# Differential attention of a decoder trunk: scaling the second map and adding the maps as one VectorE operation

## The reference, cut to what matters

```python
s = jnp.einsum('bqhme,bkhme->bhmqk', q2, k2).astype(jnp.float32) * (A_HD ** -0.5)
s = jnp.where(dist >= 0, s + bias[:, None], -jnp.inf)
p = jax.nn.softmax(s, axis=-1)
w = p[:, :, 0] - lam * p[:, :, 1]
return jnp.einsum('bhqk,bkhe->bqhe', w, v.astype(jnp.float32))
```

## Time and profile before

| what | value |
|---|---|
| median of three runs | 3593.33 us |
| the profiled execution, its own time | 3596.45 us |
| its span | 3594.9 us |
| granted PE clock, mean over the span | 0.969 |
| busy over the span: PE, DVE, ACT, POOL | 91%, 53%, 38%, 14% |

### The profile page before, as it was taken

One profiled execution on the slowest core, in us unless ns is written; L12 is line 12 of the kernel. 1 busy time (PEld: TensorE's weight loads), 2 busy tenths in 40 slices (PEclk: granted clock), 3 DMA queues, 4 the chain that ended last, 5 costly groups with the idle time before them and its releaser, 6 DMA issues. The chain is left out here.

```text
span 3594.9 us, 58426 instructions
## 1 busy us (share of the span) xinstructions
PE 3268.0 (91%) x19347; PEld 3022.6 (84%) x19347; DVE 1909.9 (53%) x4454; ACT 1378.7 (38%) x2979; POOL 516.2 (14%) x397
## 2 busy tenths in 40 slices
PE   6999999688889998688599699999999999999997
PEld 5999999577779997344488599999999999999997
DVE  5222222466668875233598465376366537636754
ACT  5111111377766775222344233333333333333332
POOL 0011011144430001233254000010010001001000
PEclk9999999899999999899799899999999999999999
DMA  4333334633537666999476676467447647644342
GB/s 131 112 106 104 108 121 132 174 72 84 111 77 167 168 171 184 283 318 302 165 246 208 186 230 210 118 214 231 142 149 252 197 123 225 218 147 145 117 116 83
DMA packets 642920, 597.48 MB, mean 166 GB/s; under 512 B 42729, under 2 KB 565442, under 8 KB 637570
## 3 DMA queue, kind: packets, MB, share of 16 engines
q1 hardware_dynamic: 610806, 461.86, 45.1%
q10 hardware_dynamic: 12814, 70.05, 5.6%
q0 software_dynamic: 19104, 63.06, 5.3%
HBM read 492.42 MB, written 169.68 MB: 184 GB/s over the span
## 5 line engine op out<-in xcount | busy, mean ns | idle before, releaser
L2358 DVE TENSOR_TENSOR ff_wl<-ff_wr,ff_wh 128x1024 fp32r<-128x1024 f32 (+2 forms) x380 | 404.1, 1079 | 283.4 <-ACT ff_wh L2290 282.3
L2290 ACT ACTIVATE ff_wh<-ff_wr 128x1024 fp32r<-128x1024 f32 (+2 forms) x380 | 349.5, 939 | 245.7 <-PE ff_d L2218 123.5
L450 PE MATMUL pj_acc<-hT_h,pj_wh 128*128 128x416 f32 x960 | 339.6, 354 | 10.1 <-POOL pj_wl L367 10.1
L450 PE MATMUL pj_acc<-hT_l,pj_wh 128*128 128x416 f32 x960 | 337.5, 352 | 0.0
L2216 PE MATMUL ff_g<-ff_hh,ff_wh 128*128 128x416 f32 x880 | 309.7, 352 | 26.8 <-DMA ff_hh<-scratch_h2T 23.7
L2216 PE MATMUL ff_u<-ff_hh,ff_wh 128*128 128x416 f32 x880 | 310.8, 353 | 16.5 <-DVE ff_wl L2358 16.5
L2216 PE MATMUL ff_d<-ff_ah,ff_wh 128*128 128x416 f32 x880 | 313.2, 356 | 9.4 <-DVE ff_wl L2358 9.4
L2218 PE MATMUL ff_d<-ff_ah,ff_wl 128*128 128x416 f32 x880 | 310.8, 353 | 0.0
L2218 PE MATMUL ff_g<-ff_hh,ff_wl 128*128 128x416 f32 x880 | 310.6, 353 | 0.0
L2218 PE MATMUL ff_u<-ff_hh,ff_wl 128*128 128x416 f32 x880 | 310.4, 353 | 0.0
L2217 PE MATMUL ff_g<-ff_hh,ff_wh 128*128 128x416 f32 x880 | 308.4, 350 | 0.1
(11 more groups left out here) (266 smaller groups left out, 7079.0 us busy)
## 6 DMA issues: line engine op xcount, KB each, us to landing
ff_wr<-in_w_gate SPq DMA_DIRECT2D x110, 512.0 KB, 4.1
ff_wr<-in_w_up SPq DMA_DIRECT2D x110, 512.0 KB, 5.0
bx_kca<-in_cache_a_k SPq DMA_DIRECT2D x128, 256.0 KB, 10.5
sa_vca<-in_cache_a_v POOLq DMA_DIRECT2D x128, 256.0 KB, 7.2
out<-in_cache_win_k ACTq DMA_DIRECT2D x64, 511.0 KB, 4.7
out<-in_cache_win_v ACTq DMA_DIRECT2D x64, 511.0 KB, 4.7
ff_wr<-in_w_down SPq DMA_DIRECT2D x80, 384.0 KB, 4.0
ff_wr<-in_w_down SPq DMA_DIRECT2D x80, 320.0 KB, 3.5
```

Source lines behind the costliest of these rows:

```text
L450: m = pe.matmul(acc[g][:, 0:PG], weights[:, k, c], part[:, c, cols], start=start, stop=stop)
L2290: act.activation(wh[:, slot, 0:size], wr[:, slot, 0:size], ACT.Copy).then_inc(w_hi, 1)
L2358: dve.tensor_tensor(wl[:, slot, 0:size], wr[:, slot, 0:size], wh[:, slot, 0:size].bitcast(F32), ALU.subtract).then_inc(w_lo, 1)
```

## The change

`scale` and the POOL block are gone, and with them the semaphore `p2_ok`. In their place DVE does `combine(x-1)` right behind `factors(x-1)`: p1 = p2 * c2 + p1, one `scalar_tensor_tensor` over all the tile's keys, in place in p1. It raises `w_ok`, for which the same consumers wait as before: `turn` on PE, and DVE's own `add_bias` and `factors` for the buffers `p2` and `c2`.

```diff
+            def combine(x):
+                n = keys(x)
+                dve.wait_ge(c2_ok, raised(x + 1))
+                dve.scalar_tensor_tensor(p1[:, x % R1, 0:n], p2[:, x % R2, 0:n], c2[:, x % 4:x % 4 + 1], p1[:, x % R1, 0:n],
+                                         ALU.mult, ALU.add).then_inc(w_ok, 1)
+
@@ DVE's list
                         negate_max(x)
                         if x >= 1:
                             factors(x - 1)
+                            combine(x - 1)
                 if x == NX:
                     factors(x - 1)
+                    combine(x - 1)
...
-        @block.gpsimd
-        def _(pool):
-            for x in range(NX):
-                n = keys(x)
-                w, y = p1[:, x % R1, 0:n], p2[:, x % R2, 0:n]
-                pool.wait_ge(p2_ok, raised(x + 1))
-                pool.tensor_tensor(w, w, y, ALU.add).then_inc(w_ok, 1)
...
-            def scale(x):
-                y = p2[:, x % R2, 0:keys(x)]
-                act.wait_ge(c2_ok, raised(x + 1))
-                act.activation(y, y, ACT.Copy, scale=c2[:, x % 4:x % 4 + 1]).then_inc(p2_ok, 1)
-
@@ ACT's list
             for x in range(NX + LAG):
                 n = parts(x - LAG)
-                if 0 <= x - 2 < NX:
-                    scale(x - 2)
```

More of the change, by code:

```diff
@@ L527, in attend_a @@
         o_out = [s.sem(f"o_out{i}") for i in range(2)]
-        (scored, biased, max_ok, exp_ok, rl_ok, c2_ok, p2_ok, w_ok, turned, wt_act, wt_dve, pv, o_ok) = (
-            s.sem(n) for n in ("scored", "biased", "max_ok", "exp_ok", "rl_ok", "c2_ok", "p2_ok", "w_ok", "turned",
+        (scored, biased, max_ok, exp_ok, rl_ok, c2_ok, w_ok, turned, wt_act, wt_dve, pv, o_ok) = (
+            s.sem(n) for n in ("scored", "biased", "max_ok", "exp_ok", "rl_ok", "c2_ok", "w_ok", "turned",
                                "wt_act", "wt_dve", "pv", "o_ok"))
```

## The result

The changed kernel took 3632.58 us (median of four runs, 3629.0 to 3635.0), the kernel before 3594.34 us in the same comparison (four runs). The ratio is 1.0109 with a 95% interval of 1.0096 to 1.0122: slower by 38 us. The forecast was 3632 us. The sum behind that number was not as good as the number, as the stretches show.

A forecast was written before the change was run, and what follows sets the result against it. In attention A's tiles 4 to 15 PE leads and DVE follows closely. Floor 29.8, unusable waits 10.5, between heads 0 and end -1.4 sum to 38.9 us, giving 3632 us; range 3609 to 3666 us.

The forecast's parts named there:

- DVE's list paces the tiles 4 to 15: Attention A, long stretches: DVE would use up its waits and be the later engine, busy 95% or more in tiles 9-11.
- The price of combine: DVE's new operation: 1.04 ns an element plus 0.22 us, about 1.3 us in the mean, 86 us busy.
- If every wait of DVE in these tiles is used up ... a head grows by 16.7 less its waits: Floor for tiles 4 to 15 (head 0: 9 to 15): 4.9, 8.5, 8.6 and 7.8 us by head, together 29.8 us.
- Neither sets the pace in these tiles: Tiles 4 to 15: removing ACT's 77.1 us and POOL's 161.1 us gives back only part of DVE's 8.9 us waits.
- PE's stop before a group that DVE copies: Waits DVE can't use: about 5 us in head 2, 1.5 in head 1, 1 in others; 10.5 us with tiles 8-11.
- the walk: Tile 13 stepped through from combine's end: DVE waits nothing, 0.3 or 1.45 us as it copies group 2, 1 or 0.
- rival B: Tiles 4 to 15: DVE's waits stay and combine comes on top; 3654 us, to 3680 with PE's lower clock; chance 0.18.
- Between heads: Three passages: products 0.8 us later each, 2.4 us, against 2.4 us from one c2 operation; sum 0, bounds -6 to +6.
- The tiles before head 0's query load cost nothing, the end gives 1.4 us: Head 0's early growth, some 3 us, only shortens the load wait; without POOL the stage's end comes 1.4 us sooner.
- The checks named: Changed profile: DVE's exponential waits under 25 us, no score waits in head 3's long tiles, PE's score-bank waits new and large.
- C: Rival: the loop through factors, scale and POOL paces the tiles, DVE's 90.6 us of waits cover combine; 3585 us, chance 0.09.
- D: Rival: combine runs at two elements a cycle, halving 1.04 ns; 3602 us, chance 0.07.

The follow-up runs named there:

- e4: The changed kernel with combine over only the first half of a tile's keys; 3596.64 us (ratio 1.0005).
- e11: The changed kernel with every copy of transposed maps on ACT, and finish on ACT too; 3553.72 us (ratio 0.9906).
- e7: The kernel before without ACT's scale pass, the factor left out and POOL's sum waiting for c2 alone; 3576.06 us (ratio 0.9948).
- e1: The changed kernel with every copy of transposed maps on ACT, none on DVE; 3562.87 us (ratio 0.9927).
- e10: The kernel before, scale on ACT and sum on POOL, with every copy of transposed maps on ACT; 3585.13 us (ratio 0.9980).
- e2: The changed kernel with DVE's copies counted anew in each head, every head as head 0; 3610.71 us (ratio 1.0071).
- e3: The changed kernel with DVE's copies in every head as in head 2, group 0 in the long tiles; 3658.81 us (ratio 1.0189).
- e6: The kernel before with only POOL's sum moved to DVE, behind the first map's adds, scale staying on ACT; 3617.86 us (ratio 1.0068).
- e12: e11 with combine in pieces of 512 keys, each releasing its own group of transposes; 3552.02 us (ratio 0.9891).
- e5: The changed kernel with PE repeating score chunk 3's two matmuls three more times in head 2's tiles 12 to 15; 3627.37 us (1.0117).

## Why the prediction was right or wrong

- *DVE's list paces the tiles 4 to 15.* Right in heads 0, 1 and 3, and shown: DVE is busy 96 to 98% of them (86% in head 2). In head 3 its waits fell from 8.9 to 0.5 us, and the length of combine (e4) and the 0.26 us of finish (e11) come out again in tiles 4 to 11.
- *The price of combine.* Right: 1.352 us in the mean, 86.5 us in all; I had about 1.3 and 86. The c2 operation starts at 1064.30 in head 3, combine at 1064.56 and the next add 2.00 us after that, with 1792 keys; the sum had 0.26 and 2.00 us:

```profile
1064.30 0.22 DVE L738 SCALAR_TENSOR_TENSOR aa_c<-aa_ll,aa_nlam,aa_rl 128x1 f32<-128x1 f32 x1
1064.56 2.08 DVE L744 SCALAR_TENSOR_TENSOR aa_p<-aa_p,aa_c 128x1792 f32<-128x1792 f32 x1
1066.56 0.68 DVE L715 CUSTOM_DVE_ANT_0 aa_p<-aa_sc,aa_bias 128x512 f32<-128x512 f32 x1
```

- *"If every wait of DVE in these tiles is used up ... a head grows by 16.7 less its waits".* This term was too large: 4.9, 8.5 and 7.8 us for heads 0, 1 and 3 as a floor, and measured 2.7, 6.8 and 4.6 in all. I took the idle time that the waits view doesn't list (0.15 us a tile) as fixed and the busy time as incompressible. Both gave way. An add that follows another at once takes 0.61 us of the list; one followed by a wait shows 0.69, and it is the whole 0.69 that counts as busy. In head 3, 16.7 us of list went into 4.6 us of growth, so 12.2 us were found, more than the 10.7 us of idle time: busy time grew by 13.6 us (54.31 to 67.88), and the idle time fell by 9.0. All of the growth lies in tiles 4 to 11 (34.25 to 38.82 us); the long tiles took 30.78 us before and 30.76 after, because before something else held them up (the next point).
- *"Neither sets the pace in these tiles", of ACT and POOL.* Wrong for ACT. Without its pass the tiles 4 to 15 were 4.1, 2.4 and 4.0 us shorter in heads 1 to 3 (e7), although has only 1.2 us of waits for exponentials, and PE's matmuls waited 0.8 us for copies by ACT in head 3's long tiles. What I had left out are the waits of PE's weight loads (PEld). In the kernel before, head 3, the first row is of tiles 12 to 15, the second of tiles 4 to 11:

```profile
PEld aa_ob L673 <- ACT aa_wt L802: 2.6, 7, 0.7
```

```profile
PEld aa_tb L660 <- POOL aa_p L773: 3.3, 4, 1.2
```

  The same rows in e7: none, and 1.4 us. So the products stood behind ACT's copies, and the transposes behind POOL's sum, which itself waited for ACT's pass. How the 4.0 us divide between the two no run separates, because e7 also lets POOL start sooner. The long tiles of e1 and e10 fit this: 28.8 us without such waits for ACT, 30.8 us with 3.0 us of them.
- *PE's stop before a group that DVE copies.* Right in kind, head by head, before any run (e2 and e3 confirm it), and near in size in head 2 (+16.6, forecast +14.4). But there two errors met: the order costs 11.1 us (81.03 against 69.93 in e2), where I had about 5, and the list 5.5 us (69.93 against 64.44), where I had 8.6. In head 1 the order costs 1.7 us (71.80 against 70.07), where I had 1.5. The stop itself is in the timeline of PE, tile 13 of head 2:

```profile
942.89 1.16 PE L673 MATMUL aa_ob<-aa_vv,aa_wt 128*128 128x128 f32 x8 [2.04 <-DVE aa_wt L724]
943.80 0.91 PE L648 MATMUL aa_sc<-bx_kk,aa_qq 128*128 128x512 f32 x2
944.51 0.84 PE L660 MATMUL aa_tb<-bx_ident,aa_p 128*128 128x128 f32 x3
945.01 1.20 PE L648 MATMUL aa_sc<-bx_kk,aa_qq 128*128 128x512 f32 x2
946.00 1.80 PE L673 MATMUL aa_ob<-aa_vv,aa_wt 128*128 128x128 f32 x8
```

  What the walk lacked is what follows the stop: a pair of score matmuls takes 1.20 instead of 0.71 us and eight products 1.80 instead of 1.06. I had the lower clock only as part of rival B. DVE's waits in head 2's long tiles were 2.0 us a tile in the mean (1.36, 2.87, 2.83, 1.00), not 1.45.
- *Between heads: 0.* Wrong, +5.3 us: -0.4, +1.9 and +3.8. The sum left out which groups DVE copies: in e2, where every head has head 0's pattern, the passages differ from the kernel before by -0.4, -0.6 and +0.1 us. The first passage came out as the walk had it: factors 1.7 us earlier in the iteration, the copy at 766.33 behind 2.27 us of combine, and the products 0.7 us later in the passage (I had 0.8). PE's stop before that copy grew from 3.91 to 6.29 us, since PE also got there sooner. The one c2 operation that took 2.64 us has none like it now (all 64 have a mean of 220 ns).

```profile
767.07 2.08 PE L673 MATMUL aa_ob<-aa_vv,aa_wt 128*128 128x128 f32 x8 [6.29 <-DVE aa_wt L724]
```

- *The tiles before head 0's query load cost nothing, the end gives 1.4 us.* Right: the wait for the load fell from 7.69 to 5.4 us on DVE, the tiles up to 8 came out 0.6 us shorter, and the end gave 1.8.
- *The total.* 33.6 us in the stage against 38.9, and 4.0 us behind it in the profiled pair, which is within the spread of the later stages. The mechanism was right, but that the forecast met the median to 1 us was luck: three heads were overrated by about 12 us, and head 2, the passages and the later stages made up 11 to 12.
- *The checks named.* DVE's wait for exponentials under 25 us, no waits for scores in head 3, the growth of PE's waits: right. But the larger new wait of PE is for DVE's copies (17.1 to 49.1 us), not for the scores' banks (11.5 to 23.9, of which 10.6 are the wait at the start of the stage in both).
- *The rivals.* C, that the loop through scale and POOL is the limit, falls as a forecast: the loop's waits did not cover combine. It holds in part for the kernel before, where e7 shows that ACT's pass, and with it the start of POOL's sum, cost 4.0 us in head 3. Taking the sum off POOL does not pay by itself: with it alone moved (e6) the kernel is slower by 0.7%. B, waits unchanged, holds in head 2 alone. D falls by the price.

The version that beats both kernels is e12 or e11: 3552 and 3554 us, 1.1 and 0.9% under the kernel before.

## What to carry to other kernels

A share of busy time below 100% in an in-order list is not slack that a new long instruction can use: ask what the engine does for others behind it. Here a costly part was a 0.6 us copy queued behind a 2 us sum, for which another engine stood still, and its place in a rotation decided 9.6 us a head. Work taken off an engine (ACT's 77 us) is worth more once something is given to it in exchange: moved together with the copies, the same change is about 20 us faster instead of 38 us slower. To see who holds PE up, read the waits of its weight loads too, and not those of its matmuls alone. And a total that fits is no proof of its terms: compare them one by one.

## What the runs showed of the hardware

PE fell to the lower of its two levels (2.4 and 1.2 GHz) after stops of only 2 us, with 7 to 9.5 us between them in which it waited for nobody. In head 2's long tiles of the changed kernel this followed two of four stops, those of 2.04 and 1.95 us, and not those of 0.65 and 1.78; the granted clock was 0.83 from 941 to 951 us and 0.91 over the four tiles. In head 3's long tiles of e3, with stops of 1.80, 2.03, 1.95 and 1.76 us, it followed the second alone (0.57 from 1075 to 1079 us), and the four tiles had 0.96. What decides between the two I did not find out. Filling the stops with repeated matmuls (e5) left 1.31, 0.90 and 0.38 us of them and brought 1.00.

```profile
941.00:951.00 10.00, 8.11 (x45) 7.24 (x46) 7.03 (x23) 3.81 (x5) 0.00 (x0) 0.83 0.00 0
```
